# The modulation's product moved from VectorE to fp32 column-group matmuls on TensorE, and every low part of a weight made on VectorE

## The reference

```python
def first_block(x, ...):                       # two layers, then a final norm
    x = x + conformer_conv(rmsnorm(x), ...)    # 1024 -> 2048, GLU, depthwise conv of 31, layernorm, 1024 -> 1024
    x = x + swiglu(rmsnorm(x), ...)            # (silu(h @ w_gate) * (h @ w_up)) @ w_down, 1024 -> 2816 -> 1024
    x = x + dilated_attention(rmsnorm(x), ...) # three head groups of different dilation
    x = x + swiglu(rmsnorm(x), ...)
    return rmsnorm(x)

def second_block(x, c, ada_w, ada_b, ...):
    cond = jax.nn.silu(c)                      # (1, 1024)
    for l in range(2):
        mod = cond @ ada_w[l] + ada_b[l]       # (1, 1024) @ (1024, 6144)
        sh1, sc1, g1, sh2, sc2, g2 = split(mod, 6)
        h = _rms_norm(x, norm_mix[l]) * (1.0 + sc1) + sh1
        x = x + g1 * (mixer_l(h) @ w_out[l])   # l = 0: differential and top-k sparse attention; l = 1: window of 128
        h = _rms_norm(x, norm_ffn[l]) * (1.0 + sc2) + sh2
        x = x + g2 * swiglu(h, ...)
    return x
```

## Time and profile before

| | |
|---|---|
| time, median of 3 runs | 1421.95 us (1414.31 to 1422.16) |
| the profiled execution | 1414.15 us, of which the span from first to last instruction is 1412.9 us |
| mean granted TensorE clock in it | 0.942 of full speed |
| TensorE busy | 1230.7 us (87%), 9796 products |
| VectorE busy | 983.8 us (70%), 1672 instructions |
| ScalarE, GpSimd busy | 653.7 us (46%), 588.0 us (42%) |

### The profile page before, as it was taken

One profiled execution on the slowest core, in us unless ns is written; L12 is line 12 of the kernel. 1 busy time (PEld: TensorE's weight loads), 2 busy tenths in 40 slices (PEclk: granted clock), 3 DMA queues, 4 the chain that ended last, 5 costly groups with the idle time before them and its releaser, 6 DMA issues.

```text
span 1412.9 us, 24775 instructions
## 1 busy us (share of the span) xinstructions
PE 1230.7 (87%) x9796; PEld 1164.9 (82%) x9796; DVE 983.8 (70%) x1672; ACT 653.7 (46%) x1139; POOL 588.0 (42%) x294
## 2 busy tenths in 40 slices
PE   5888897998998997998898677969699968799999
PEld 4868897897987997988897567969699856799999
DVE  5966799887465899887679646989644543575532
ACT  5326544443445544435456654333344664454441
POOL 4413544346421544336553235333256433444442
PEclk9999999998999999999999898989899988899999
DMA  7577777676642477676543214768556430465662
GB/s 256 150 179 130 233 269 268 223 285 210 215 150 90 150 272 257 234 255 222 205 135 116 75 32 146 264 247 272 176 171 206 158 105 30 123 206 180 181 192 75
DMA packets 81126, 259.36 MB, mean 184 GB/s; under 512 B 8904, under 2 KB 20424, under 8 KB 81012
## 3 DMA queue, kind: packets, MB, share of 16 engines
q1 hardware_dynamic: 81012, 257.79, 56.3%
HBM read 252.68 MB, written 5.08 MB: 182 GB/s over the span
## 4 chain that ended last, share of the span: by engine, by line
PE 45%; DVE 30%; issue 14%; ACT 4%; POOL 2%; DMA 2%; DVEq 0%; SPq 0%; ACTq 0%; POOLq 0%
PE ps L508 38%; DVE aacc L1172 6%; DVE wlo L1166 5%; DVE tmp L1166 3%; DVE GL L1166 2%; DVE CV L1172 2%; PE ps L602 1%; PE ps L567 1%; POOL oS L1697 1%; DMA raw<-wall 1%; PE ps L606 1%; ACT HH L815 1%; DVE aacc L1169 1%; PE ps L598 1%; DVE RST L1219 1%
## 5 line engine op out<-in xcount | busy, mean ns | idle before, releaser
L1697 POOL TENSOR_TENSOR wlo<-raw,whi 128x1024 fp32r<-128x1024 f32 x188 | 499.6, 2660 | 629.2 <-ACT whi L815 629.2
L508 PE MATMUL ps<-HH,whi 128*128 128x256 f32 (+1 forms) x2152 | 629.4, 292 | 57.2 <-DVE HL L1166 29.8
L508 PE MATMUL ps<-HL,whi 128*128 128x256 f32 (+1 forms) x2152 | 618.6, 287 | 0.0
L508 PE MATMUL ps<-HH,wlo 128*128 128x256 f32 (+1 forms) x2152 | 618.6, 287 | 0.0
L508 PEld LDWEIGHTS ps<-HH,whi 128*128 128x128 f32 x2152 | 420.1, 195 | 77.4 <-ACT HH L815 35.1
L815 ACT ACTIVATE whi<-raw 128x1024 fp32r<-128x1024 f32 x363 | 375.7, 1051 | 227.4 <-PE ps L508 221.9
L508 PEld LDWEIGHTS ps<-HL,whi 128*128 128x128 f32 x2152 | 420.0, 195 | 0.4
L508 PEld LDWEIGHTS ps<-HH,wlo 128*128 128x128 f32 x2152 | 419.4, 195 | 0.0
L1166 DVE TENSOR_TENSOR wlo<-raw,whi 128x1024 fp32r<-128x1024 f32 x175 | 269.2, 1539 | 65.9 <-ACT whi L815 65.9
L1172 DVE SCALAR_TENSOR_TENSOR aacc<-araw,cond,aacc 128x512 f32<-128x512 f32 x168 | 206.7, 1230 | 3.4
L508 PE MATMUL ps<-GH,whi 128*128 128x256 f32 x704 | 200.9, 285 | 6.6 <-DVE tmp L1166 5.8
(11 more groups left out here) (209 smaller groups left out, 1123.0 us busy)
## 6 DMA issues: line engine op xcount, KB each, us to landing
raw<-wall SPq DMA_DIRECT2D x363, 512.0 KB, 4.1
araw<-ada SPq DMA_DIRECT2D x96, 512.0 KB, 4.5
UR<-uscr SPq DMA_DIRECT2D x24, 142.0 KB, 3.2
scratch<-bvec SPq DMA_DIRECT2D x1, 3072.0 KB
oBB<-kbias SPq DMA_DIRECT2D x16, 192.0 KB, 2.9
aTB<-scratch SPq DMA_DIRECT2D x12, 128.0 KB, 2.3
X<-x_in SPq DMA_DIRECT2D x2, 512.0 KB, 5.8
out<-X SPq DMA_DIRECT2D x8, 128.0 KB, 3.2
```

Source lines behind the costliest of these rows:

```text
L508: ins = pe.e.matmul(o, l, r, start=(kt == p.order[0] and i == 0), stop=(kt == p.order[-1] and i == 2))
L1697: po.then_inc(po.e.tensor_tensor(o, a, b, op), sem)
```

## The change

The accumulation on VectorE, its accumulators and `number_ada` go. The modulation becomes 48 sets of four fp32 products on TensorE: cond, widened to 32 equal columns, is the stationary operand, 512 columns of ada weights the moving one, and the four products of a set write the four groups of 32 partitions of PSUM bank 6, accumulating over the 8 row tiles. So 8 sets give 2048 columns of the modulation, six times. Sets stand behind tiles 1, 5, ..., 41 of gu0, gu1 and gu2 and behind tiles 2, 3, 4, 5 and 5 of dn0, dn1 and dn2; a set reads two loads of 512 KB (araw now has 5 buffers), which SyncE issues one set ahead. The copy to arow, the turn and the addition of ada_b remain, behind every eighth set. The gains that need the modulation are made in three pieces, as their parts are ready.

At the same time GpSimd makes no low parts of weights any more; VectorE makes all 363, in order, under one semaphore `lo`. GpSimd keeps its normalisation tiles, the squares and two steps of the mixers.

```diff
-ARAW = 3
-AACC = 5
+ARAW = 5
 ADA_COLS = 512
-ADA_K = 2
+ADA_CHUNKS = 2
+N_SETS = 2 * 6 * D // (4 * ADA_COLS) * KD
...
-def pool_makes(v):
...
-def number_ada():
...
+SET_TILES = [(f"{a}{f}", nt) for f in range(3) for a, at in (("gu", range(1, 42, 4)), ("dn", (2, 3, 4, 5, 5))) for nt in at]
+SUM_AT = {SET_TILES[KD * b + KD - 1]: b for b in range(N_SETS // KD)}
+TURN_AT = {(name, nt + 1): b for (name, nt), b in SUM_AT.items()}
...
                     pe.wait_ge(S.hi, u + 1)
-                    pe.wait_ge(*low_at(u))
+                    pe.wait_ge(S.lo, u + 1)
...
             def sums(name, nt):
-                if (name, nt) in SUM_AT:
-                    b = SUM_AT[name, nt]
-                    pe.wait_ge(S.ada, 8 * ADA_PARTS * (b + 1))
-                    if b:
-                        pe.wait_ge(S.amod, b)
-                    for i in range(4):
-                        ins = pe.e.matmul(bank[6][32 * i:32 * i + 32, :], ones[:, 0:32], aacc[(4 * b + i) % AACC][:, :],
-                                          start=True, stop=True)
-                    pe.then_inc(ins, S.asum)
+                for n, at in enumerate(SET_TILES):
+                    if at == (name, nt):
+                        b, kt = divmod(n, KD)
+                        pe.wait_ge(S.cond, 1)
+                        if b and kt == 0:
+                            pe.wait_ge(S.amod, b)
+                        for i in range(4):
+                            v = 2 * n + i // 2
+                            pe.wait_ge(S.ara[v % ARAW], 16 * (v // ARAW + 1))
+                            ins = pe.e.matmul(bank[6][32 * i:32 * i + 32, :], cond[:, kt, :],
+                                              araw[v % ARAW][:, i % 2 * ADA_COLS:(i % 2 + 1) * ADA_COLS],
+                                              start=(kt == 0), stop=(kt == KD - 1))
+                        pe.then_inc(ins, S.ada)
...
-                act(cond[:, :], vec[:, VCOL["c"]:VCOL["c"] + 8], ACT.Silu, S.cond)
+                act(cond[:, :, :], vec[:, VCOL["c"]:VCOL["c"] + 8].unsqueeze(2).broadcast_to([P, KD, 32]), ACT.Silu, S.cond)
...
             def lows(upto):                                   # VectorE
                 for v in range(made[0], upto + 1):
-                    if not pool_makes(v):
-                        dv.wait_ge(S.hi, v + 1)
-                        tt(wlo[v % RING][:, :], raw[v % RAW][:, :], whi[v % RING][:, :].bitcast(F32), ALU.subtract, S.lov)
-                    for _ in range(ADA_AFTER.get(v, 0)):
-                        ada_step()
+                    dv.wait_ge(S.hi, v + 1)
+                    tt(wlo[v % RING][:, :], raw[v % RAW][:, :], whi[v % RING][:, :].bitcast(F32), ALU.subtract, S.lo)
...
                     j = 7 if i is None else i - 1
+                    if j >= 4:
+                        dv.wait_ge(S.amod, {4: 2, 5: 3, 6: 5, 7: 6}[j])
...
-            def lows(upto):                                   # GpSimd
-                for v in range(made[0], upto + 1):
-                    if pool_makes(v):
-                        po.wait_ge(S.hi, v + 1)
-                        tt(wlo[v % RING][:, :], raw[v % RAW][:, :], whi[v % RING][:, :].bitcast(F32), ALU.subtract, S.lop)
...
                     if v >= RAW:                              # SyncE
-                        sp.wait_ge(*low_at(v - RAW))
+                        sp.wait_ge(S.lo, v - RAW + 1)
                     load(raw[v % RAW][:, :], wall[v], S.raw[v % RAW])
...
+            def load_set(n):
+                for v in (2 * n, 2 * n + 1):
                     if v >= ARAW:
-                        sp.wait_ge(S.ada, 2 * (v - ARAW + 1))
+                        sp.wait_ge(S.ada, (v - ARAW) // 2 + 1)
                     load(araw[v % ARAW][:, :], ada[v], S.ara[v % ARAW])
...
             def rest(name):
                 for nt in range(PROD[name].tiles):
                     lows(low_to(name, nt))
+                    for n, at in enumerate(SET_TILES[:-1]):
+                        if at == (name, nt):
+                            load_set(n + 1)
```

More of the change, by code:

```diff
@@ L136, in low_to @@
     return v if v == N_UNITS - 1 else v - 1
-def pool_makes(v):
[L141 to L149, removed]
-def number_ada():
[L154 to L194, removed]
+SET_TILES = [(f"{a}{f}", nt) for f in range(3) for a, at in (("gu", range(1, 42, 4)), ("dn", (2, 3, 4, 5, 5))) for nt in at]
+assert len(SET_TILES) == N_SETS
+SUM_AT = {SET_TILES[KD * b + KD - 1]: b for b in range(N_SETS // KD)}
+TURN_AT = {(name, nt + 1): b for (name, nt), b in SUM_AT.items()}
 AFTER_D = {6: [("score", 0)], 7: [("score", 1), ("exp", 0)], 8: [("log", 0), ("exp", 1)], 9: [("share", 0), ("log", 1)],
@@ L395, in program @@
             msk, bvec = sb("msk", [12, 512], F32, st), sb("bvec", [12, 512], F32, st)
-        araw = [sb(f"araw{i}", [P, ADA_K * ADA_COLS]) for i in range(ARAW)]
-        aacc = [sb(f"aacc{i}", [P, ADA_COLS]) for i in range(AACC)]
+        araw = [sb(f"araw{i}", [P, ADA_CHUNKS * ADA_COLS]) for i in range(ARAW)]
         arow = sb("arow", [P, ADA_COLS])
@@ L1172, in stt @@
                 dv.then_inc(dv.e.scalar_tensor_tensor(out=o, in0=a, scalar=s, in1=b, op0=op, op1=op2), sem)
[L1174 to L1186, removed]
-                        ts(a[:, :], src, cond[:, 0:1], None, ALU.mult, None, S.ada)
-                    else:
-                        dv.wait_ge(S.ada, 2 * v + i)
-                        stt(a[:, :], src, cond[:, kt:kt + 1], a[:, :], ALU.mult, ALU.add, S.ada)
             def lows(upto):
                 for v in range(made[0], upto + 1):
-                    if not pool_makes(v):
-                        dv.wait_ge(S.hi, v + 1)
-                        tt(wlo[v % RING][:, :], raw[v % RAW][:, :], whi[v % RING][:, :].bitcast(F32), ALU.subtract, S.lov)
-                    for _ in range(ADA_AFTER.get(v, 0)):
-                        ada_step()
+                    dv.wait_ge(S.hi, v + 1)
+                    tt(wlo[v % RING][:, :], raw[v % RAW][:, :], whi[v % RING][:, :].bitcast(F32), ALU.subtract, S.lo)
                 made[0] = max(made[0], upto + 1)
@@ L1776, in odd_step @@
                     factors(oS[hp % 3], oST[hp % 3][:, 3, :], S.osp)
-            feed_forward(0)
-            for nt in range(18):
-                if nt - 1 not in PROD["mixd"].double:
-                    lows(low_to("mixd", nt))
-            residual("outd", 3)
-            feed_forward(1)
-            residual("oute", 5, projection("mixe", AFTER_E, even_step))
-            feed_forward(2)
-            residual("outo", 7, projection("mixo", AFTER_O, odd_step))
-            feed_forward(3)
+            for kt in range(KD):
+                norm_lows(0, kt)
+            for kt in range(KD):
+                added(0, kt)
+            residual("pw2", 1)
+            residual("dn0", 2)
+            residual("outd", 3)
+            residual("dn1", 4)
+            for x in STEPS_E:
+                even_step(*x)
+            residual("oute", 5)
+            residual("dn2", 6)
+            for x in STEPS_O:
+                odd_step(*x)
+            residual("outo", 7)
         def sync_program():
             sp = Queue(nc.sync)
-            loaded, ada_loaded, stepped = [0], [0], [0]
+            loaded, stepped = [0], [0]
             def load(o, i, sem):
```

101 lines of the change are left out of this document (29 added, 72 removed).

## The result

The changed kernel takes 1381.37 us in the median of four runs (1380.07 to 1384.25), the kernel before 1418.2 (four runs, 1414.31 to 1422.16): a ratio of 0.974, 95% interval 0.970 to 0.978. The forecast was 1377, with a range of 1355 to 1407. The profiled execution took 1380.07 us with a span of 1378.7; before, 1414.15 and 1412.9.

The account below looks back on a forecast made before the run. Feed-forward stages were taken as bound by TensorE, except where it waits for VectorE's accumulation. -82 + 53 + 4 + 0 - 12 - 5 = -42 us gave 1372 from the profiled execution, 1380 from the median; forecast 1377, range 1355 to 1407.

Parts of the forecast that it names:

- Sums removed, -82: Modulated feed-forwards: removing VectorE's accumulation and TensorE's six waits for it saves 82 us, priced by stages without modulation.
- Sets added, +53: Feed-forward stages: 48 sets on TensorE's path at 1.1 us each add 53 us, bounds 42 and 93.
- The rival of sets at 1.93 us: Sets run at half clock and cost as the old sum's row did, so the change buys nothing: 1417 us, chance 0.07.
- The second set of tile 5, +4: dn0, dn1, dn2: TensorE waits about 1.5 us for this set's late loads, three times, 4 us; bounds 0 and 26.
- The rival of the sets that wait for their loads: TensorE waits at each set for its loads; gain gone from 0.9 us a set, 1473 us at 2 us; chance 0.05.
- All low parts on VectorE: VectorE takes over GpSimd's 188 low parts at 1.22 us each, 229 us; in gu3 still hidden under TensorE.
- Mixer E, 0: Mixer E: 18 low parts taken over, 22 us, against stretching that goes; taken as 0, bounds +22 and -15.
- First product, -5: First product: VectorE takes over 8 low parts but loses stretched instructions, a gain of 5 us; bounds -7 and +10.
- Two ends, -12: Ends of oute and outo: VectorE keeps up, so TensorE's waits for normalised tiles shrink, gaining 12 us; bounds 0 and 13.

Follow-up runs that it names:

- e3: The changed kernel with the second set behind tile 5 of each down product moved behind tile 6: 1363.05 us, ratio 0.961.
- e2: The kernel before with all low parts made by VectorE and none by GpSimd, the modulation still accumulated on VectorE: 1333.36 us, ratio 0.940.
- e1: The changed kernel with low parts again made by VectorE and GpSimd in turn, so the sets alone: 1411.37 us, ratio 0.996 to the kernel before.
- e5b: e2 with each sum of the modulation placed one tile later: 1318.97 us, ratio 0.931 to the kernel before.
- e4: The changed kernel with 42 of its 48 sets cut to the first 32 of 512 columns: 1362.11 us, ratio 0.960.
- e6: e2 with GpSimd doing idle subtractions that nobody reads where it made low parts before: 1391.55 us, ratio 0.982 to the kernel before.
- e8: The kernel before with each of GpSimd's 188 low parts cut into four subtractions of 128x256: 1356.67 us, ratio 0.960.

## Why the prediction was right, step by step

The number held, and so did most terms. One thing it did not see is that its two halves remove the same waits. Its price for the waits comes from stages that have no modulation, so it holds whichever half removes them; the reason that it gave did not hold. That the total came so near is in part luck, since two terms that were too hopeful met small gains that were not forecast (below).

*Sums removed, -82.* The six feed-forward stages of e3, where the sets do not wait, take 640.5 us; less 48 x 1.09 that is 588, against 587.4 + 5 forecast. Right, and 4 us too small. But the prediction gave these waits to the accumulation as work, 135 - 76 = 59 us a stage, and e2 shows that the work was not the trouble: the accumulation, at 770 ns an instruction, and all low parts fit beside TensorE, in 114 of gu1's 127.6 us. The rows for this were in hand: the prediction priced the stretching of VectorE's instructions beside GpSimd in the mixers, at the ends of products and in the first product, and not in the feed-forward stages, which had GpSimd's low parts too and the largest waits. By its terms the low parts alone would have been worth 12 + 5 = 17 us and the sets alone 82 - 53 - 4 = 25. Measured were 83 (e2) and 5 (e1).

*Sets added, +53.* Right: 48 x 1.09 = 52 us, at granted clock 1.00 (1.19 a set by e5b's gu1). The rival of sets at 1.93 us did not come true. Here the Trainium skill's figure for column tiles, in "TensorE: Matmul & The Clock Gate", Part 3, was weighed; a set by it would have streamed 1.15 us, my estimate from that page. The rows of e4 put 512 columns in four groups at 0.85 us, near the 0.88 from the convolution; the measurement decides.

*The second set of tile 5, +4.* The step that was mis-sized: it cost 18 us, by e3, inside its bounds of 0 to 26. The prediction had the loads issued 3 us ahead and landing in 4.5. The timeline of SyncE in dn1 and the loads issued from 648 to 658 us (KB each, median us to landing) show both wrong:

```profile
650.70 2.84 SPq L1691 DMA_DIRECT2D araw<-ada  x4
```

```profile
araw<-ada SPq DMA_DIRECT2D x4, 512.0 KB, 7.4
```

They go out 1.4 us ahead of the first set (652.09), four at once and behind weight loads. And the idling costs twice, as the sums' had: the window around the pair has a granted clock of 0.85 and only 4.38 us of TensorE, the one ahead of it 1.00.

```profile
640.00:650.00 10.00, 10.00 (x85) 1.00 0.90 317
652.00:660.50 8.50, 4.38 (x19) 0.85 0.90 352
```

The rival of the sets that wait for their loads thus came true at these three places; spread over 48 sets it is 0.4 us a set, where the rival needed 0.9 to undo the gain.

*All low parts on VectorE.* Right: 1.22 us in the median, 1.77 at the most, hidden under TensorE in gu1 to gu3. *Mixer E, 0:* a gain of 4.2 us, inside its bounds (no working stands behind the lower one, a gain of 15). *First product, -5:* 5.2. It is the low parts' alone: pw1 takes 104.6 us in e1 and 98.8 in e2.

*Two ends, -12.* The waits fell as forecast, from 9.4 and 9.08 to 2.3 us, 13.9 in all, but the stages got only 1.0 (oute) and 4.3 us (outo) shorter. In oute the clock gave it back:

```profile
807.90:864.10 56.20, 38.01 (x275) 32.23 (x273) 33.86 (x56) 28.81 (x71) 24.66 (x21) 0.89 0.22 67
```

```profile
792.00:847.20 55.20, 42.74 (x275) 35.87 (x273) 29.27 (x61) 28.98 (x71) 18.25 (x17) 0.82 0.25 71
```

The first is oute before, the second after: the same 275 records take 4.7 us more on TensorE, at a mean granted clock of 0.82 in place of 0.89. Why the clock is lower there, no run tells.

The sum by stage: -16.0 in the six feed-forward stages (-82 - 4 + 52 + 18), -5.2, -5.3 at the ends, -4.2 in mixer E and -3.7 in all others, -34.4 in all; the spans differ by 34.2. The terms that missed, +14 (loads) and +7 (ends), were partly met by gains not foreseen, 4 us each in three places: the sums, mixer E and the remaining stages.

Two things stay open. Of the 83 us that GpSimd's low parts cost, how much is VectorE's standing still was not separated from the rest. e6 costs 58 us, but it is no part of the 83: VectorE makes all 363 low parts there, and the idle subtractions are shorter. That the results came late from GpSimd is not the larger part, since a low part takes GpSimd 4 x 0.96 = 3.8 us in e8 against 2.66 in the mean before, and e8 is 58 us faster; 23 us above e2 remain in it. And e1 is slower than before by some 8 us outside the feed-forward stages (pw2 3.3, oute 3.9, mixd 1.8), for which I have no row.

## What to carry to other kernels

When an engine shows up as late, compare the duration of its own instructions with the shortest of the same form before its work is moved elsewhere: here the work was affordable and the neighbour made it dear. When a change has two halves, run each alone; a right total can hide that one half carries the gain and the other spends part of it. A late load in a stage bound by TensorE is worth a place of its own: three sets, each moved by one tile, were 18 us.

## What the runs showed of the hardware that was not expected

Beside a subtraction on GpSimd, a VectorE instruction with both inputs in SBUF is not slowed in proportion, but stands until the GpSimd instruction is over: GL, 0.42 us by itself, ends 0.28 to 0.29 us behind it, 32 times before and 78 times in e8. So it is held up for less than one GpSimd instruction: 2.2 us beside low parts of 2.34 us at the least (before), 0.58 us beside quarters of 0.72 (e8), 0.28 us beside idle subtractions of 0.54 in the median (e6). An instruction with one input in PSUM is not held up at all (tmp<-ps,RST, 426 ns at the most). So the same elements cut in four cost 58 us less in this kernel, though GpSimd is then busy for 781.8 us and not 588.0. The Trainium skill, "SBUF — State Buffer", section "Who interferes with whom", says that the two engines share a pair of ports as an exclusive lock, held for the whole instruction; these rows agree with it, since the wait lasts until the GpSimd instruction ends and not longer.
